# A fused two-block transformer kernel: the normalised input starts at another column of its buffers in each of six stages

## What is computed

```
h = rms_norm(x, g_pre) * (1 + scale) + shift     # the normalised input
y = f_s(h)
x = x + gate * rms_norm(y, g_post)
```

## Time and profile before

| | |
|---|---|
| time, median of 3 runs | 997.55 us (996.96 to 998.17) |
| the profiled execution | 997.55 us, of it 995.7 us from the first to the last instruction |
| granted TensorE clock, mean | 0.996 |
| instructions | 19,019, of them 6,806 matmuls and as many weight loads |
| moved by DMA | 234.08 MB |

### The profile page before, as it was taken

How to read it: one execution, slowest core, us unless ns; L and a number is a source line. 1 busy time by engine, 2 the same in 40 slices (tenths; PEclk the granted TensorE clock), 3 DMA queues, 4 the chain that set the end, 5 groups by cost and what they waited for, 6 DMA issues and landing times. The chain is left out here.

```text
span 995.7 us, 19019 instructions
## 1 busy us (share of the span) xinstructions
PE 963.3 (97%) x6806; PEld 886.0 (89%) x6806; DVE 821.5 (83%) x1217; ACT 543.3 (55%) x1023; POOL 77.9 (8%) x111
## 2 busy tenths in 40 slices
PE   4899999999999999998999999999999999999997
PEld 3899988999999888996999999989997899999996
DVE  4869978887777778777988777789998989987885
ACT  3455546544444467555644444459998555555452
POOL 2100002000000012011300000002240000000000
PEclk9999999999999999999999999999999999999999
DMA  9999973999999965652599999985340649766641
GB/s 347 327 339 336 337 256 108 349 348 318 312 312 310 285 190 162 179 176 79 174 354 347 317 312 308 314 258 170 86 127 1 201 133 286 225 187 183 183 121 42
DMA packets 240770, 234.08 MB, mean 235 GB/s; under 512 B 7497, under 2 KB 208970, under 8 KB 240714
## 3 DMA queue, kind: packets, MB, share of 16 engines
q1 hardware_dynamic: 237824, 226.52, 73.8%
q0 software_dynamic: 1616, 5.32, 1.6%
q10 hardware_dynamic: 1274, 1.52, 0.4%
HBM read 232.27 MB, written 1.06 MB: 234 GB/s over the span
## 5 line engine op out<-in xcount | busy, mean ns | idle before, releaser
L1341 DVE TENSOR_TENSOR wlo<-raw,whi 128x1024 fp32r<-128x1024 f32 x286 | 346.7, 1222 | 67.4 <-ACT whi L999 67.2
L527 PE MATMUL work<-h_hi,whi 128*128 128x256 f32 x1360 | 383.1, 282 | 2.0 <-DVE h_lo L1402 1.9
L527 PE MATMUL work<-h_hi,wlo 128*128 128x256 f32 x1360 | 381.0, 280 | 0.0
L527 PE MATMUL work<-h_lo,whi 128*128 128x256 f32 x1360 | 380.8, 280 | 0.0
L999 ACT ACTIVATE whi<-raw 128x1024 fp32r<-128x1024 f32 x286 | 297.7, 1053 | 143.5 <-PE work L527 45.4
L527 PEld LDWEIGHTS work<-h_hi,whi 128*128 128x128 f32 x1360 | 256.5, 189 | 5.4 <-issue 2.0
L527 PEld LDWEIGHTS work<-h_lo,whi 128*128 128x128 f32 x1360 | 256.1, 188 | 3.1
L527 PEld LDWEIGHTS work<-h_hi,wlo 128*128 128x128 f32 x1360 | 257.0, 189 | 0.0
L1351 DVE SCALAR_TENSOR_TENSOR acc<-ada_raw,csil,acc 128x1024 f32 (+1 forms) x128 | 163.7, 1280 | 6.1 <-DMA ada_raw<-in_ada_w 4.4
L564 PE MATMUL Y<-whi,ab_hi 128*128 128x512 f32 x286 | 90.0, 395 | 0.0
L564 PE MATMUL Y<-whi,ab_lo 128*128 128x512 f32 x286 | 89.8, 395 | 0.0
(11 more groups left out here) (226 smaller groups left out, 1323.8 us busy)
## 6 DMA issues: line engine op xcount, KB each, us to landing
ada_raw<-in_ada_w SPq DMA_DIRECT2D x88, 512.0 KB, 6.5
raw<-in_ffn_w_in SPq DMA_DIRECT2D x88, 512.0 KB, 7.6
ada_raw<-in_mod_w SPq DMA_DIRECT2D x48, 512.0 KB, 6.8
raw<-in_ffn_w_out SPq DMA_DIRECT2D x44, 512.0 KB, 5.7
raw<-in_f_up_w SPq DMA_DIRECT2D x44, 512.0 KB, 4.0
raw<-in_moba_w_qkv SPq DMA_DIRECT2D x24, 512.0 KB, 8.3
raw<-in_diff_w_qkv SPq DMA_DIRECT2D x24, 512.0 KB, 7.8
raw<-in_a_pw_w SPq DMA_DIRECT2D x24, 512.0 KB, 6.5
```

The lines of the kernel that those rows point to most:

```text
L527: mm = pe.matmul(dst, w[:, u, ws], h[:, k, :], start=(k == 0 and m == 0), stop=(k == KT - 1 and m == 2))
L1341: dve.tensor_tensor(wlo[:, u, :], raw[:, u, :], whi[:, u, :].bitcast(F32), ALU.subtract).then_inc(lo[u], 1)
```

## The change

Each stage takes its views of `h_hi` and `h_lo` at another column: stage s begins 16 s columns (64 s bytes) into both buffers. The buffers grow by 80 columns each (320 bytes), and `small` shrinks from 96 to 64 columns, so all that is declared after `h_hi` moves: `h_lo` by 320 bytes, `head_bias` and the rest up to `small` by 640 bytes, what follows by 512. Sizes, shapes and orders of the instructions, and all waits, are as they were.

```diff
+H_AT = {0: 0, 1: 16, 2: 32, 3: 48, 4: 64, 5: 80}
+H_ROOM = 80
...
-        h_hi = sb("h_hi", [P, KT, S], F32R)
-        h_lo = sb("h_lo", [P, KT, S], F32R)
+        h_hi = sb("h_hi", [P, KT * S + H_ROOM], F32R)
+        h_lo = sb("h_lo", [P, KT * S + H_ROOM], F32R)
...
-        small = sb("small", [P, 96])
+        small = sb("small", [P, 64])
...
+        h_at = {s: [h[:, at:at + KT * S].rearrange("p (k n) -> p k n", k=KT) for h in (h_hi, h_lo)]
+                for s, at in H_AT.items()}
...
-            def col_product(dst, u, n, early=None, before=None):
+            def col_product(s, dst, u, n, early=None, before=None):
+                hh, hl = h_at[s]
...
-                    for m, (w, h) in enumerate(((whi, h_hi), (whi, h_lo), (wlo, h_hi))):
+                    for m, (w, h) in enumerate(((whi, hh), (whi, hl), (wlo, hh))):
...
-                            for m, (h, w) in enumerate(((h_hi, whi), (h_lo, whi), (h_hi, wlo))):
+                            for m, (h, w) in enumerate(((hh, whi), (hl, whi), (hh, wlo))):
...
-                            row_tile(h_hi[:, k, :], h_lo[:, k, :], 4 + 2 * (r % 2) + j,
+                            row_tile(h_at[4][0][:, k, :], h_at[4][1][:, k, :], 4 + 2 * (r % 2) + j,
...
-                    act.activation(h_hi[:, k0:k1, :], x_parts(s, k0, k1), ACT.Copy).then_inc(hhi, 1)
+                    act.activation(h_at[s][0][:, k0:k1, :], x_parts(s, k0, k1), ACT.Copy).then_inc(hhi, 1)
...
-                    dve.tensor_tensor(h_lo[:, k0:k1, :], x_parts(s, k0, k1), h_hi[:, k0:k1, :].bitcast(F32),
+                    dve.tensor_tensor(h_at[s][1][:, k0:k1, :], x_parts(s, k0, k1), h_at[s][0][:, k0:k1, :].bitcast(F32),
```

More of the change, by code:

```diff
@@ L774, in step @@
                     else:
-                        col_product(work[:, 0, 0:S], j, i + nb, s if n == 0 else None, used[4] if j else None)
+                        col_product(s, work[:, 0, 0:S], j, i + nb, s if n == 0 else None, used[4] if j else None)
                         if s == 0:
@@ L779, in step @@
                             need(pe, sb_done, n * 2 + HEADS[2])
-                        col_product(work[:, 3, 0:S], 2 + j, i + nb)
+                        col_product(s, work[:, 3, 0:S], 2 + j, i + nb)
                     if n >= lag:
@@ L843, in products @@
                             pe.wait_ge(gate_done, before + fb)
-                    col_product(work[:, 2 * j, 0:S], j, i + nb)
+                    col_product(s, work[:, 2 * j, 0:S], j, i + nb)
                     if not start:
@@ L849, in products @@
                             pe.wait_ge(act_done, before + fb)
-                    col_product(work[:, 2 * j + 1, 0:S], 2 + j, i + nb)
+                    col_product(s, work[:, 2 * j + 1, 0:S], 2 + j, i + nb)
                 products(0, 0)
@@ L872, in conformer @@
             def conformer():
-                nb, fb = USE[4][0], STEPS[4]
+                s, nb, fb = 4, USE[4][0], STEPS[4]
                 def conv(i, j, half_way=None):
@@ L1300, in conformer @@
                     hs = slice(ks[0], ks[-1] + 1)
-                    act.activation(h_hi[:, hs, :], convT[:, hs, :], ACT.Copy).then_inc(p_hi, 1)
+                    act.activation(h_at[4][0][:, hs, :], convT[:, hs, :], ACT.Copy).then_inc(p_hi, 1)
                 prep(1, NI_C + nb)
@@ L1841, in low_group @@
                     dve.wait_ge(p_hi, n + 1)
-                    dve.tensor_tensor(h_lo[:, hs, :], convT[:, hs, :], h_hi[:, hs, :].bitcast(F32),
+                    dve.tensor_tensor(h_at[4][1][:, hs, :], convT[:, hs, :], h_at[4][0][:, hs, :].bitcast(F32),
                                       ALU.subtract).then_inc(p_lo, 1)
```

## The result

The changed kernel takes **1005.09 us** (median of 4 runs, 1004.61 to 1005.68) against 997.62 us for the kernel before beside it (median of 4, 996.96 to 998.17): ratio 1.0075, 95% interval 1.0063 to 1.0087. It is 7.5 us slower. The forecast was 997.5 us, with a range that ended at 1003.

A forecast was written before the change was run, and what follows sets the result against it. PE's own pace was taken to bound the kernel. All address moves were put at 0 us, so 995.7 + 0 = 995.7 us, with 1.85 us outside the span 997.55 us; range 990 to 1003 us.

The forecast's parts named there:

- The bound: Whole kernel: PE's own pace sets the time, no wait does; PE busy 963.3 of 995.7 us.
- Step (a): Moving operand of L527 and L545 starts 64 s bytes further on in stage s: 0 us, between 18.7 won and 8.5 lost.
- The upper bound: Most that moved starts could cost, from the convolution's pitch: 1.8 ns for each of 4,704 matmuls, 8.5 us lost.
- Step (b): `values` (L750) and 84 matmuls of L564 take `h` as stationary operand: 0 us by the same reasoning.
- Step (c): `ab` and others move by 640 bytes: first half, even steps gain, 0.7 us won; second, as much lost; taken as 0.
- Step (d): DVE and ACT write `h` with the same shapes, on the path only at a stage's start: 0 us.
- Step (e): PE's state on entering a stretch sets the short pitch: 1.5 us slower or faster, the width of no change.
- The slower one: Rival: streams beginning in the same 64 bytes of a 256-byte stretch collide, stage 3 worst; 5 us, 1002.5 us; chance 0.20.
- The faster one: Rival: some new starts let PE run at the short pitch; 7 us won, 990.5 us; chance 0.25.
- no change: Likeliest case for the whole kernel: moved addresses are indifferent, 995.5 to 999.5 us; chance 0.55.
- The sign that I had set: Forecast is wrong if L527's mean differs between stages 1, 3 and 5 by over 0.5 ns.

The follow-up runs named there:

- the kernel of 983 us: Against the kernel before: `h` at distance 192 from the weights in all stages, second channel tile of `ab` beginning 320 columns after the first; 983.16 us, ratio 0.9876.
- Columns only: Against the changed kernel: buffers grow by 64 columns, keeping all places modulo 256 bytes; stages start at columns 0, 16, 32, 48, 64, 32; 998.37 us, ratio 1.0004.
- column 32: Against the changed kernel: all stages start at column 32, all else in its place modulo 256 bytes; 989.59 us, ratio 0.9912.

## Why the prediction was wrong

**The bound: right.** PE's pace sets the time. Span less PE's busy time is 32.4 us before and after, so the loss is PE's work and no wait. In the kernel of 983 us it is 33.9 us, and 1.1 us of what was added is one row product in stage 3 that waits for DVE's `ab_lo`; the DMA share of 0.97 in stage 1 held nothing back. One reading was too coarse: the slices of the earlier trace rows show the clock as 9 throughout, but the trace has 3.4 us at 0.50 from 766.5 us on.

**Step (a): wrong, and the step that failed.** It put the cost of the moved starts at 0, and they cost 7.4 us in the column products of stages 1, 3 and 5 alone. The rows showed moves by 256 and 512 bytes to be indifferent, and that was right: stages 256 bytes apart have equal patterns, and with `h_lo` and all behind it moved by multiples of 256 bytes ("Columns only") stages 0 and 4, at distance (64, 64), kept 116.7 and 117.8 ns. What I made of it, 0 for moves by 64, 128 and 192 bytes, had no row. That the pace is the same 256 bytes on says nothing of what lies between. Measured there: -2.3 to +3.2 ns per column product. The upper bound, 1.8 ns from the convolution's mean, was too low as well; its row holds only starts within 48 bytes of each other.

**Step (b):** the same error, +0.9 us for `values`. **Step (c):** the row products won 1.4 us, within twice its bound of 0.7, and in sign as its first half said; that `ab` alone did it is not shown, since with `ab` in the same place they took 232.3 ns at (192, 192). **Step (d)** held. **Step (e):** the pace at entry is real. In stages 0 and 2 the short pitch of before was lost, for which 1.5 us had been allowed; 1.7 us were lost there with `values`. Its reach was underrated: at (192, 192) it alone decides between 113.9 and 117.8 ns as the mean of a stage, and without the right entry that distance gives stages 1, 3 and 5 next to nothing.

**The rivals.** The slower one had the right kind of mechanism, two streams and their distance modulo 256, and gave 1002.5 us against 1005.1. Its rule was wrong: a start in the same 64 bytes is not the worst case. Stage 3, with `h_hi` at distance 0, lost least of the three (0.9 us), and stages 1 and 5, at (128, 192), lost 3.4 and 3.1 us; distance (0, 0) in every stage cost 5.5 us, less than the change did. That its time came near is in part luck, as its 5 us was a choice between 1.9 and 8.5. The faster one was no less true: column 32 has it, 8 us, but in this change it fell to stage 2, where `h_lo` stood at 0 and not at 192 beside it. The chances gave both together 0.45; with one period shown and its inside untested that was too little, and 0.55 for no change too much. The sign that I had set, a difference of over 0.5 ns between stages 1, 3 and 5, told the miss at once: 124.3, 122.0 and 124.1 ns.

## What to carry to other kernels

Where PE is the bound and its stream is dense, compare its pitch over a whole stretch, and look whether the same instructions show two pitches in one trace; if they do, the placement of the operands is worth a scan. One run with another start in each repeated stage, read by stage and not by its total, shows several placements at once; a total of "no change" can hold one stage that is 2 us better beside two that are worse. Choose the places of neighbouring products' operands jointly, as the pace of one stream depends on the one ahead of it: at (192, 192) for `h`, 64 bytes in the place of `ab` were worth 9 us.

## What the runs showed of the hardware

- The pitch of PE's fp32r matmuls depends on the distance between the moving operand and the weights modulo 256 bytes. At 256 columns it is 113.9 ns at best and 121.0 at worst as the mean of stage 1, 3 or 5, at 512 columns 227 to 233 ns. The Trainium skill, SBUF — State Buffer, section "Who interferes with whom", gives PE two independent read ports and says that it never waits. These traces don't agree: with the weights moved by 64 bytes against `h`, at equal work, the kernel is 5.5 us slower, and with both moved it is not.
- One pair of distances can have two lasting paces. At (64, 64) and at (192, 192) a stretch settles within some six matmuls at 113.3 or at 117.8 ns and stays there for all 48; at (0, 64), stage 3 of the changed kernel, the stretches alternate between 117.8 and 120.0 ns. 113.3 ns are 272 cycles of 2.4 GHz for 256 columns, 226.7 ns, the lowest row products, 544 for 512: both 17 for 16 columns.
- Which of the two a stretch takes follows the place of `ab`, the stationary operand of the row product ahead: 64 bytes there, with `h` and the weights where they were, turn 113.3 into 117.8 ns (983.16 and 992.11 us). What else lies behind `h_lo` moved too; that it is `ab` is argued from the paces' alternation with its even and odd tiles.
- Open: what in the chip has the period of 256 bytes, whether the distance between `h_hi` and `h_lo` counts beside their distances from the weights, and by what rule the entry picks the pace. Distances that are no multiple of 64 bytes were not scanned for `h`.
